# Parting the latents' 672 weight columns at 384 instead of 512, and making the second rotary table later

## The reference, cut to what matters

```
xn = rmsnorm(x, norm_mix_g)
proj = xn @ w_in
q_lat, kv_lat, k_rope, dq, dk, dv, gate_pre = split(proj, [384, 256, 32, 512, 512, 512, 2048])
q  = rmsnorm(q_lat, mla_q_norm_g) @ mla_w_uq        # 8 heads x (64 plain + 32 rotary)
kv = rmsnorm(kv_lat, mla_kv_norm_g) @ mla_w_ukv     # 8 heads x (64 keys + 64 values)
# q's rotary part and k_rope are turned by the angles of table 1 (rope_m),
# dq and dk by the angles of table 2 (rope_d)
```

## Time and profile before

| what | value |
| --- | --- |
| time, median of 3 runs | 1302.12 us (1301.53 to 1302.45) |
| profiled execution, own time | 1302.51 us |
| its span | 1300.8 us |
| PE busy in the span | 1274.4 us, 98% |
| DVE, ACT, POOL busy | 54%, 41%, 4% |
| chain that ended last, by engine | PE 89%, DVE 6%, ACT 3% |

### The profile page before, as it was taken

One profiled execution on the slowest core, in us unless ns is written; L12 is line 12 of the kernel. 1 busy time (PEld: TensorE's weight loads), 2 busy tenths in 40 slices (PEclk: granted clock), 3 DMA queues, 4 the chain that ended last, 5 costly groups with the idle time before them and its releaser, 6 DMA issues.

```text
span 1300.8 us, 15821 instructions
## 1 busy us (share of the span) xinstructions
PE 1274.4 (98%) x6212; PEld 1062.9 (82%) x6212; DVE 700.1 (54%) x1073; ACT 527.8 (41%) x889; POOL 55.1 (4%) x97
## 2 busy tenths in 40 slices
PE   8999999999999999999999999899999999999997
PEld 6877778888888888888888888688988888888885
DVE  6776656654545444444433348756555436446554
ACT  5546554652334434343323243336553343223222
POOL 0002231220000000000000000000000000000000
PEclk9999999999999999999999999899999999999999
DMA  6232323123432332323223233231104322322321
GB/s 196 69 97 66 81 74 89 50 81 92 160 120 65 97 100 94 99 95 114 95 91 104 97 98 114 65 97 38 61 1 146 108 91 94 103 92 98 104 75 64
DMA packets 106362, 119.53 MB, mean 92 GB/s; under 512 B 13814, under 2 KB 88636, under 8 KB 106300
## 3 DMA queue, kind: packets, MB, share of 16 engines
q1 hardware_dynamic: 106160, 118.64, 29.1%
q10 hardware_dynamic: 140, 0.04, 0.0%
HBM read 113.42 MB, written 2.10 MB: 89 GB/s over the span
## 4 chain that ended last, share of the span: by engine, by line
PE 89%; DVE 6%; ACT 3%; issue 2%; POOL 1%; DVEq 0%; ACTq 0%; POOLq 0%
PE ps_mm L1930 55%; PE ps_mm L1965 22%; PE ps_o L2342 2%; PE ps_o L2117 1%; ACT w_hi L640 1%; PE ps_s L2094 1%; DVE w_lo L1150 1%; PE ps_t L2322 1%; PE ps_mm L1936 1%; PE ps_mm L2025 1%; PE ps_s L2138 1%; PE ps_t L2104 1%; PE ps_s L2307 1%; PE ps_o L2165 1%; PE ps_s L2305 1%
## 5 line engine op out<-in xcount | busy, mean ns | idle before, releaser
L1930 PE MATMUL ps_mm<-act_hi,w_hi 128*128 128x512 f32 x944 | 373.6, 396 | 5.2 <-DVE w_lo L1150 5.2
L1930 PE MATMUL ps_mm<-act_lo,w_hi 128*128 128x512 f32 x944 | 371.1, 393 | 0.0
L1930 PE MATMUL ps_mm<-act_hi,w_lo 128*128 128x512 f32 x944 | 370.9, 393 | 0.0
L1150 DVE TENSOR_TENSOR w_lo<-stage,w_hi 128x2048 fp32r<-128x2048 f32 (+3 forms) x77 | 157.7, 2048 | 173.9 <-ACT w_hi L640 173.9
L1930 PEld LDWEIGHTS ps_mm<-act_hi,w_hi 128*128 128x128 f32 x944 | 178.0, 189 | 41.5 <-DVE w_lo L1150 6.7
L1930 PEld LDWEIGHTS ps_mm<-act_hi,w_lo 128*128 128x128 f32 x944 | 177.9, 188 | 35.7
L1930 PEld LDWEIGHTS ps_mm<-act_lo,w_hi 128*128 128x128 f32 x944 | 178.0, 189 | 34.4
L640 ACT ACTIVATE w_hi<-stage 128x2048 fp32r<-128x2048 f32 (+3 forms) x78 | 133.1, 1706 | 166.6 <-PE ps_mm L1965 119.1
L1566 DVE TENSOR_TENSOR w_lo<-stage,w_hi 128x2048 fp32r<-128x2048 f32 x23 | 52.7, 2293 | 56.3 <-ACT w_hi L919 56.2
L1965 PE MATMUL ps_mm<-w_hi,h_hi 128*128 128x512 f32 x176 | 68.8, 391 | 0.0
L1965 PE MATMUL ps_mm<-w_hi,act_hi 128*128 128x512 f32 x176 | 68.6, 390 | 0.0
(11 more groups left out here) (389 smaller groups left out, 1973.9 us busy)
## 6 DMA issues: line engine op xcount, KB each, us to landing
stage<-in_w_in SPq DMA_DIRECT2D x44, 1024.0 KB, 5.3
stage<-in_w_ffn_gate SPq DMA_DIRECT2D x11, 1024.0 KB, 5.3
stage<-in_w_ffn_up SPq DMA_DIRECT2D x11, 1024.0 KB, 5.3
stage<-in_w_ffn_down SPq DMA_DIRECT2D x10, 1024.0 KB, 5.0
stage<-in_w_out SPq DMA_DIRECT2D x4, 1024.0 KB, 5.0
stage<-in_w_att_out SPq DMA_DIRECT2D x4, 1024.0 KB, 5.1
stage<-in_w_sg_out SPq DMA_DIRECT2D x4, 1024.0 KB, 5.1
stage<-in_w_o SPq DMA_DIRECT2D x4, 1024.0 KB, 5.2
```

Of the source, the lines that this page charges most:

```text
L1150: V.tensor_tensor(w_lo[:, s, 0:k * w], stage[:, s, 0:k * w], w_hi[:, s, 0:k * w].bitcast(F32), ALU.subtract).then_inc(w_lo_made, 1)
L1930: ins = T.matmul(ps_mm[:, 2 * bank_slot + m, :], wt[:, kk, m * P:(m + 1) * P], acts[ap][:, kk, :], start=(r == 0), stop=(r == per - 1), sk ...
```

## The change

The latents get four units in place of three: units 0 and 1 hold columns 0 to 383, units 2 and 3 columns 384 to 671, each pair in two halves of the contraction and each with four banks, one for each token tile. All later units and bank groups move up by one. The angles of table 2 and their sine and cosine are no longer made among the latents: DVE makes the angles after `lo` of the second query unit and before it keeps the banks of the first, and ACT makes sine and cosine after it has copied the banks of the first query unit and before `hi` of the rotary queries' unit. `lo` of the second dv unit moves behind the scaling of the latents.

```
-COUNTS = [("lat", 3), ("dv", 2), ...
+COUNTS = [("lat", 4), ("dv", 2), ...
-        _per = 0 if (_n, _i) == ("lat", 2) else WIDE.get(_n, 0)
+        _per = WIDE.get(_n, 0)
...
-                return wide(w_in, 0, i) if i < 2 else (w_in[:, :, 512:LAT], 8, LAT - 512)
+                return wide(w_in, 0, i, w=QR) if i < 2 else wide(w_in, QR, i - 2, w=LAT - QR)
...
-                cc = slice(512 * k, 512 * k + 512)
+                cc = slice(QR * k, QR * k + QR)
...
 ACT, latents
             hi(2)
             for t in range(TT):
+                if t == TT - 1:
+                    hi(3)
                 act.wait_ge(bank_free, freed(1, t))
                 latent_squares(t, t, 0, QR)
             sincos(0, rope_m)
-            hi(3)
+            hi(U0["dv"])
             for t in range(TT):
-                act.wait_ge(bank_free, freed(2, t // 2))
+                act.wait_ge(bank_free, freed(3, t))
                 latent_squares(TT + t, t, QR, QR + KVR)
-            hi(4)
-            sincos(1, rope_d)
-            hi(5)
+            hi(U0["dv"] + 1)
+            hi(U0["qn"])
 ACT, queries, after the banks of a unit v are copied
+                if v == U0["qn"]:
+                    sincos(1, rope_d)
 DVE, keep_latents(u)
+                    a, b = (0, QR) if u == 1 else (QR, LAT)
+                    V.tensor_scalar(lat[:, t, a:b], bank(u, t)[:, 0:b - a], r, None, ALU.mult).then_inc(bank_free, 1)
 DVE, latents
             lo(2)
             keep_latents(1)
+            lo(3)
             dve.wait_ge(xr_turned, 1)
...
-            angles(rope_d, 1, pos_f[:, :])
-            lo(3)
-            keep_latents(2)
-            lo(4)
+            lo(U0["dv"])
+            keep_latents(3)
...
+            lo(U0["dv"] + 1)
             lo(U0["qn"])
 DVE, queries
             for u in range(U0["qn"], U0["mv"]):
                 if u != U0["kn"]:
                     lo(u + 1)
+                if u == U0["qn"]:
+                    angles(rope_d, 1, pos_f[:, :])
 PE
-            straight(2, "T", acts_x)
+            wide_unit(2, acts_x)
+            wide_unit(3, acts_x)
```

## The result

The changed kernel takes 1305.85 us (median of 8 runs, 1304.56 to 1306.74) against 1302.05 for the kernel before, measured beside it. The ratio is 1.0027, with a 95% interval of 1.0018 to 1.0035: 2.3 to 4.6 us slower. The forecast was 1301.9 with a range up to 1304.0, so both the time and the sign were missed. Seven of the eight runs have a mean granted TensorE clock of 0.993; the eighth has 0.995 and the shortest time, 1304.56. The span grew from 1300.8 to 1304.1 us.

The account below looks back on a forecast made before the run. PE, busy 1274.4 of 1300.8 us, was taken as the bound, with DVE able to take over early. Terms -2.9 (parting), -0.2 (lighter `lo`) and +2.9 (wait at `qp`) gave -0.2, so 1301.9 us, range 1299.7 to 1304.0.

Parts of the forecast that it names:

- the refilling that was forecast: At `qp`, after PE's wait for its weights: PE's pipeline fills again, costing 0.33 us.
- The gain of the first part: From the start through the latents' units: units 2 and 3 end at 43.0 where 45.89 stood, 2.9 us gained.
- the lighter `lo`: First query unit: `lo` no longer runs beside POOL's multiplications, 0.96 us instead of 1.16, so 0.2 us more gained.
- The new wait itself: Before `qp`: PE ready at 80.1, weights at 82.65 in times of before; with refilling, cost 2.9 us.
- The hidden table: Rival at `qp`: PE doesn't wait there, the whole 3.1 us gain stays, 1299.0 us; chance 0.09.
- Held latents: Rival: DVE and ACT hold the latents longer, as when unit 1's load lands no earlier; +1.1 us, 1303.2; chance 0.2.
- The dear columns: Rival in units 2 and 3: 288 columns cost as much as 384, sum +4.6 us, 1306.7; chance 0.07.
- The margin called thinnest: Before the first dv unit: `keep_latents(3)` frees the first bank at K + 11.6, PE wants it at K + 12.9; 1.3 us.

Follow-up runs that it names:

- e3: Changed kernel plus twelve products of 512 columns into an unused bank between the second query unit and `qp`; 1303.68 us against 1303.12 for the kernel before, ratio 1.0004.
- e5: Changed kernel with POOL's two multiplications of table 2 held back until the first dk bank is swapped; 1304.67 us against 1302.77 for the kernel before, ratio 1.0013.
- e6: New parting, table 2's angles cut in two around the first dv unit's `lo` and the latents' scaling, sine and cosine behind `lt_hi`; 1300.46 us, kernel before 1302.77.
- e4: Changed kernel with ACT's sine and cosine of table 2 one unit later, behind `hi` of `qp`; 1303.54 us against 1303.12 for the kernel before, ratio 1.0007.
- e2: Kernel before with only table 2's angles, sine and cosine moved to the changed kernel's places; 1306.92 us against 1303.12, ratio 1.0038.

## Why the prediction was wrong

The frame held: the parting gains until the queries, the moved table makes PE wait for `qp`, and the wait is not absorbed. But gain and cost don't nearly cancel. Forecast were -0.2 us at `mv`, measured +2.5; of these 2.7 us one missing term makes 1.6 and mis-sized terms 1.1.

**The missing term: the clock after the pause.** The prediction said "PE waits, and fills again in 0.33 us: cost 2.9 us", and "After the start S of `qp` everything is tied to S as before". The wait was 2.84 us, so the first part stood, but the products after it ran at half clock for 3.4 us, a price that the prediction put at nothing. From the 1.92 us that the stretch from `qp` to `mv` grew, 0.33 are the refilling that was forecast and 1.59 are the clock, and e3 gives the same 1.6 by taking the pause away. With it away the ratio is 1.0004, some 1302.6 us, inside the forecast range. I had looked for a price of a pause only in the first 100 us, where the longest was 1.14 us before `mv`, and took its 0.33 for every pause. The kernel before has a longer one, 4.07 us at 833 us, with nine slow products behind it, 0.2 us too long each; that row would have warned of the term and given a size near it, 1.8 us, though for a longer pause.

**Terms mis-sized.** The gain of the first part was forecast as 2.9 us, and with the lighter `lo` 3.1; it was 2.25. The lighter `lo` came as forecast (0.96 for 1.16). Unit 1's load landed at 15.81 us, not 15.25, and so the first bank came at 30.7 instead of 30.1: 0.6 us. Products of 288 columns stood 0.133 us apart, not 0.130: 0.3 us. In e3, e5 and e6 the third unit starts at 30.52, 30.50 and 29.97 and in e4 at 31.87, though nothing was changed before it, so this term differs by up to 2 us between executions. `lo` of `qp` beside POOL took 1.40 us, not 1.16: 0.24 us, and e5 shows that it is POOL. The new wait itself was 2.82 us against 2.55 forecast (82.65 less 80.1).

**The sum again.** -2.25 + 2.82 + 0.33 + 1.59 = +2.5 us at `mv`, as the trace has it. Two steps of 0.4 us behind it, one the length of the clock's later fall and one open, make the 3.3 us of the spans. The medians differ by 3.8; the other 0.5 is not traced.

**The rivals.** The hidden table was rightly put low. Held latents happened to 0.6 of their 1.3 us. The dear columns didn't happen: 384 and 288 columns cost 0.173 and 0.133. A time above 1304.7 had been given to them alone, with 0.07. The measured 1305.85 lies there for another reason. A sum near zero with an unread price for a long pause should have had most of its width above the forecast. The margin called thinnest, before the first dv unit, held: PE had no wait there.

## What to carry to other kernels

A pause of PE costs more than its length once it is long enough for the clock to fall, so price a new wait by the rows behind a pause of like length anywhere in the trace, not by the shortest one near by. Work that has no early reader belongs in the gaps of its engine, cut in pieces if need be, and not ahead of the weights of the next unit. Where a pause can't be closed, products into an unused bank kept the clock up here, and in the kernel before they alone gained 3.0 us by the medians (1.9 by the traces), no less than the parting's 1.7.

## What the runs showed of the hardware that was not expected

- Pauses of PE of 0.64, 1.14 and 1.99 us were followed by products at their usual distance; pauses of 2.39 (e5), 2.83 (e2), 2.84 and 4.07 us were followed by 6 to 13 products at the lower clock, 0.43 us apart. After 2.39, 2.83 and 2.84 us a few products (five, two and three) still ran fast; after 4.07 us at most the first two did.
- The number of slow products behind one and the same pause of 4.07 us differed between executions, 6 (e6) to 13 (e4), which alone is 1.4 us.
- Products in `ps_mm` cost 0.0133 us over their columns at 2.4 GHz: 0.2267 us for 512, 0.1733 for 384 (8.32 us for the 48 of unit 1) and 0.1333 for 288. Those of 160 columns cost 0.111, more than this line's 0.080.
- DVE's subtraction of two SBUF tensors, 768 columns, took 0.96 us alone, 1.16 with POOL's multiplication beside it in the kernel before, and 1.40 in the changed one.
